# A feed-forward input projection in seven quadrant products in place of eight, on one Trainium2 core

## The reference, cut to what matters

```
def swiglu(h, w13, w2):
    a, g = jnp.split(h @ w13, 2, axis=-1)     # w13: 1024 x 5632
    return (jax.nn.silu(g) * a) @ w2          # w2: 2816 x 1024

def ffn_sublayer(x, mod, j, g_pre, g_post, w13, w2):
    h = modulate_in(x, g_pre, mod, j)
    return gated_residual(x, swiglu(h, w13, w2), g_post, mod, j, 0.5)
```

## Time and profile before

| | |
|---|---|
| median of 3 runs | 2567.58 us (2563.26 to 2568.49) |
| span of the profiled execution | 2563.5 us; its own device time is not listed apart from the three above |
| PE busy | 2506.9 us, 98% of the span |
| DVE, ACT, POOL busy | 57%, 27%, 6% |
| granted TensorE clock, mean | 0.995 |
| last feed-forward block on PE | from 2089.6 us to the last matmul at 2556.3 us |

### The profile page before, as it was taken

The page is one execution under the profiler, slowest core; times in us unless marked ns, Lnnn a source line. Parts: engine busy times, 40 slices in busy tenths (PEclk is TensorE's granted clock), DMA queues, the critical chain, the costliest instruction groups (busy, mean ns, idle before and its releaser), DMA issues. The chain is left out here.

```text
span 2563.5 us, 40540 instructions
## 1 busy us (share of the span) xinstructions
PE 2506.9 (98%) x15408; PEld 2327.2 (91%) x15408; DVE 1454.7 (57%) x2575; ACT 696.8 (27%) x1262; POOL 163.0 (6%) x263
## 2 busy tenths in 40 slices
PE   6999999999998999999999999999999999999998
PEld 5998999799888799989988998999899989989997
DVE  4887688734555688738867884333544453323333
ACT  4111111443445431111124111122421252111122
POOL 0000000201115100000001000000200020000001
PEclk9999999999999999999999999999999999999999
DMA  6553455333223244334442542223122312222232
GB/s 242 156 143 128 132 151 176 92 77 83 51 56 87 79 134 147 122 106 148 147 157 70 151 135 97 79 75 117 55 68 74 116 50 74 65 80 77 74 114 74
DMA packets 383576, 273.14 MB, mean 107 GB/s; under 512 B 39254, under 2 KB 354390, under 8 KB 382454
## 3 DMA queue, kind: packets, MB, share of 16 engines
q1 hardware_dynamic: 383478, 271.82, 35.3%
HBM read 267.42 MB, written 4.32 MB: 106 GB/s over the span
## 5 line engine op out<-in xcount | busy, mean ns | idle before, releaser
L1603 DVE TENSOR_TENSOR w_lo<-w_raw,w_hi 128x1024 fp32r<-128x1024 f32 (+1 forms) x401 | 398.2, 996 | 611.9 <-ACT w_hi L1130 607.4
L809 PE MATMUL psum<-hT_hi,w_hi 128*128 128x320 f32 x3040 | 692.8, 309 | 2.2 <-DVE w_lo L1603 1.4
L809 PE MATMUL psum<-hT_hi,w_lo 128*128 128x320 f32 x3040 | 692.8, 309 | 0.0
L809 PE MATMUL psum<-hT_lo,w_hi 128*128 128x320 f32 x3040 | 692.7, 309 | 0.0
L1130 ACT ACTIVATE w_hi<-w_raw 128x1024 fp32r<-128x1024 f32 (+1 forms) x401 | 349.3, 873 | 957.9 <-PE psum L809 535.8
L809 PEld LDWEIGHTS psum<-hT_hi,w_hi 128*128 128x128 f32 x3040 | 508.4, 188 | 3.7 <-issue 1.5
L809 PEld LDWEIGHTS psum<-hT_hi,w_lo 128*128 128x128 f32 x3040 | 508.4, 188 | 0.0
L809 PEld LDWEIGHTS psum<-hT_lo,w_hi 128*128 128x128 f32 x3040 | 508.0, 188 | 0.0
L1572 DVE SCALAR_TENSOR_TENSOR mod_acc<-ada_raw,cond_silu,mod_acc 128x256 f32<-128x256 f32 x896 | 365.3, 478 | 0.0
L736 PE MATMUL psum<-w_hi,act_hi 128*128 128x512 f32 x800 | 317.8, 397 | 2.8 <-DVE w_lo L1603 2.2
L737 PE MATMUL psum<-w_lo,act_hi 128*128 128x512 f32 x800 | 316.2, 395 | 0.0
(11 more groups left out here) (212 smaller groups left out, 2351.7 us busy)
## 6 DMA issues: line engine op xcount, KB each, us to landing
w_raw<-in_ffn_w_dram SPq DMA_DIRECT2D x176, 512.0 KB, 4.1
ada_raw<-in_ada_w_dram SPq DMA_DIRECT2D x128, 512.0 KB, 3.6
w_raw<-in_ffn_w_dram SPq DMA_DIRECT2D x148, 256.0 KB, 2.8
w_raw<-in_ab_w_in_dram SPq DMA_DIRECT2D x28, 512.0 KB, 4.0
w_raw<-in_sc_w_in_dram SPq DMA_DIRECT2D x24, 512.0 KB, 4.0
ada_first<-in_ada_w_dram SPq DMA_DIRECT2D x4, 2048.0 KB, 18.8
held_raw<-in_ffn_w_dram SPq DMA_DIRECT2D x28, 256.0 KB, 3.7
gate<-modulation SPq DMA_DIRECT2D x6, 1024.0 KB, 6.3
```

Of the source, the lines that this page charges most:

```text
L809: last = mm(IN[p][0:width, h, 0:HT], a, b[:, k, h * HT:(h + 1) * HT], start=(k == 0 and a is hi and b is hT_hi), stop=(k == KD - 1 and a i ...
L1603: V.tensor_tensor(d_, a, b.bitcast(F32), ALU.subtract).then_inc(w_lo_ok, 1)
```

## The change

In the last feed-forward block 3 of the 22 pairs stay as they were (the first three of the first half) and 19 are done in another form, called groups here, 8 in the first half and 11 in the second. The two units of a pair are taken as a 2x2 block matrix (unit by half of the 1024 inputs, each quadrant 4 slices of 128x128), the activations as another (half of the inputs by half of the tokens). Winograd's form of Strassen's product needs 7 products of quadrants, each 4 x 3 = 12 matmuls of 320 columns, and sums before and after.

- **Sums of the weights**: 4 a group, 128x512 on DVE (`weight_sums`). The split becomes 7 copies of 128x512 on ACT (`prod_split`) and 7 subtractions of 128x512 on DVE (`prod_rest`).
- **Sums of the activations**: once, beside the 3 plain pairs: 2 additions of 128x1280 on POOL, 6 sums and 4 subtractions on DVE, 4 copies on ACT.
- **Sums of the results**: of the 7 products, 3 go on top of a bank that holds an earlier one. ACT copies product 0 out (`keep_one`), DVE adds product 1 (`add_two`), product 2 (`add_five`) and product 3 (`add_seven`), then adds into the two crossing quarters (`cross`). Silu is two ACT instructions of 320; then one product, one copy and one subtraction of 640.
- **Waits on PE**: product 4 waits for `add_two` of its own group, product 5 for `add_five`, product 6 for `add_seven`.
- **Memory**: the activation sums take the place of `X`. x is written to device memory (5 transfers of 512 KB) beside the second plain pair and read back in the last output projection. The gate tile's place holds the first three products' weights, so the gate rows are loaded only after the last product.

Of the two loops over `g` in the diff the first is ACT's, the second DVE's.

```diff
+            def pair_products(s, ph, g):
+                b = banks(ph, g)
+                new = g - ph["g0"]
+                for q in range(SEVEN):
+                    pe.wait_ge(prod_lo_ok, SEVEN * g + q + 1)
...
+                    elif q == 4:
+                        pe.wait_ge(q_summed, U_TWO(g))
+                    elif q == 5:
+                        pe.wait_ge(q_summed, U_FIVE(g))
+                    else:
+                        pe.wait_ge(q_summed, U_SEVEN(g))
+                    out = PS[:, b[ACCUM[q]], 0:HT]
...
+                    for k in range(KH):
+                        on = dict(skip_group_check=q >= 4)
+                        mm(out, hi[:, k, :], o_hi[:, k, :], start=(k == 0 and q < 4), stop=False, **on)
+                        mm(out, hi[:, k, :], o_lo[:, k, :], start=False, stop=False, **on)
+                        last = mm(out, lo[:, k, :], o_hi[:, k, :], start=False, stop=(k == KH - 1), **on)
+                    last.then_inc(pe_prod, 1)
...
+            def prod_split(ph, g, q):
+                act.wait_ge(pair_loaded[g % 2][0 if q in (0, 4) else 1], 16 * (g // 2 + 1))
+                if SUMS[q]:
+                    act.wait_ge(ws_ok, 4 * g + SUMS[q])
+                need(act, pe_prod, SEVEN * (g - 1) + q + 1 if g else 0)
...
+                A(prod_hi(q), FACTOR[q](g), ACT.Copy).then_inc(prod_hi_ok, 1)
...
+                for g in range(g0, g1):
+                    more = g + 1 < g1
+                    if more:
+                        prod_split(ph, g + 1, 0)
+                    if g > g0:
+                        keep_hi(ph, g - 1)
+                        keep_one(ph, g)
+                    if more:
+                        for q in (1, 2, 3):
+                            prod_split(ph, g + 1, q)
+                    silu_one(ph, g)
+                    if more:
+                        for q in (4, 5, 6):
+                            prod_split(ph, g + 1, q)
+                    else:
+                        split(ph["nout"], shape="out", prod=slot_done(ph, 0))
+                    silu_two(g)
+                keep_hi(ph, g1 - 1)
...
+            def weight_sums(g, q):
+                if q == 1:
...
+                    V.tensor_tensor(S1[:], A21(g), A22(g), ALU.add).then_inc(ws_ok, 1)
+                    dve.wait_ge(ws_ok, 4 * g + 1)
+                    V.tensor_tensor(S2[:], S1[:], A11(g), ALU.subtract).then_inc(ws_ok, 1)
+                elif q == 3:
+                    V.tensor_tensor(A21(g), A11(g), A21(g), ALU.subtract).then_inc(ws_ok, 1)
+                elif q == 5:
+                    V.tensor_tensor(S2[:], A12(g), S2[:], ALU.subtract).then_inc(ws_ok, 1)
...
+                for g in range(g0, g1):
+                    more = g + 1 < g1
+                    if more:
+                        prod_rest(g + 1, 0)
+                        weight_sums(g + 1, 1)
+                    if g > g0:
+                        product(g - 1)
+                    if more:
+                        prod_rest(g + 1, 1)
+                    if g > g0:
+                        keep_lo(ph, g - 1)
+                        add_two(ph, g)
+                    if more:
+                        prod_rest(g + 1, 2)
+                    if g > g0:
+                        add_five(ph, g)
+                    if more:
+                        weight_sums(g + 1, 3)
+                        prod_rest(g + 1, 3)
+                    add_seven(ph, g)
+                    if more:
+                        prod_rest(g + 1, 4)
+                        weight_sums(g + 1, 5)
+                        prod_rest(g + 1, 5)
+                    else:
+                        split(ph["nout"], shape="out")
+                    cross(ph, g)
+                    if more:
+                        prod_rest(g + 1, 6)
+                product(g1 - 1)
+                keep_lo(ph, g1 - 1)
```

More of the change, by code:

```diff
@@ L80 @@
 LATE = (3, 0)
-UB = [sum(COUNT[k] for k in SUBS[:s]) for s in range(len(SUBS) + 1)]
+units_of = lambda s: COUNT[SUBS[s]] - (2 * (2 * HF - sum(PLAIN[s])) if s in PLAIN else 0)
+UB = [sum(units_of(q) for q in range(s)) for s in range(len(SUBS) + 1)]
 class Steps:
@@ L1093, in _ @@
                 for z, ph in enumerate(plan[s]):
-                    if kind == "ffn":
+                    if s in PLAIN:
+                        for i in range(1, ph["plain"]):
+                            in_unit(ph, 0, i, 2)
+                            in_unit(ph, 1, i, 2)
+                        for g in range(ph["g0"], ph["g1"]):
+                            pair_products(s, ph, g)
+                        out_phase(s, ph, ACT_HI, ACT_LO)
+                    elif kind == "ffn":
                         if z:
@@ L1233, in out_splits @@
                 for u in range(AB_SPLIT if ph.get("ab") else 1, len(units)):
-                    split(ph["nout"] + u, shape="out", u=u)
+                    split(ph["nout"] + u, shape="out", u=u, prod=slot_done(ph, u) if seven(ph) and u < 4 else 0)
                     for i in range(ph["held"]):
@@ L1240, in out_splits @@
                         square_out(s, 0, t)
-                if not final:
+                elif s in PLAIN:
+                    for q in range(3):
+                        prod_split(plan[s][1], plan[s][1]["g0"], q)
+                else:
                     split(ph["nout"] + len(units))
+            def prod_split(ph, g, q):
[3 more added lines that the diff above has]
+                need(act, pe_prod, SEVEN * (g - 1) + q + 1 if g else 0)
+                if g == ph["g0"] and q >= 3:
+                    act.wait_ge(pe_unit, slot_unit(ph, q))
+                A(prod_hi(q), FACTOR[q](g), ACT.Copy).then_inc(prod_hi_ok, 1)
@@ new lines, in t_split, with keep_one @@
+            def t_split(s, ph, i):
+                act.wait_ge(t_sum, 6 * FI[s] + (2, 3, 4, 6)[i])
+                if i in (1, 2):
+                    act.wait_ge(y_stored, 16 * NT * (FI[s] + 1))
+                if i == 3:
+                    act.wait_ge(pe_unit, ph["nout"])
+                A(T_HI[i], tsum[i][:], ACT.Copy).then_inc(t_hi, 1)
+            def keep_one(ph, g):
+                act.wait_ge(pe_prod, SEVEN * g + 1)
+                if g:
+                    act.wait_ge(q_summed, U_CROSS(g - 1))
+                A(U2[:], PS[:, banks(ph, g)[0], 0:HT], ACT.Copy).then_inc(q_gated, 1)
@@ new lines, in silu_one, with silu_two, keep_hi @@
+            def silu_one(ph, g):
+                act.wait_ge(pe_prod, SEVEN * g + 5)
+                if g > 0:
+                    act.wait_ge(q_summed, U_PRODUCT(g - 1))
+                A(Z[:, 0, :], PS[:, banks(ph, g)[0], 0:HT], ACT.Silu).then_inc(q_gated, 1)
+            def silu_two(g):
+                act.wait_ge(q_summed, U_CROSS(g))
+                A(Z[:, 1, :], Z[:, 1, :], ACT.Silu).then_inc(q_gated, 1)
+            def keep_hi(ph, g):
+                act.wait_ge(q_summed, U_PRODUCT(g))
+                j = HF - ph["g1"] + g
+                A(halves(act_hi[:, j, :]), Z[:, 2:4, :], ACT.Copy).then_inc(q_gated, 1)
@@ new lines, in mixed_in @@
+            def mixed_in(s, ph):
+                nb, g0, g1 = ph["nin"], ph["g0"], ph["g1"]
+                for i in range(ph["plain"]):
+                    if i:
+                        split(nb + 1 + 2 * i)
+                    if i == ph["plain"] - 1:
+                        for q in range(3):
+                            prod_split(ph, g0, q)
+                    act.wait_ge(pe_unit, nb + 1 + 2 * i)
+                    need(act, in_evac[(nb + 1) % 2], inv(ph, nb + 1) - 1 + i)
+                    A(halves(sg[:]), IN_V[nb % 2], ACT.Silu).then_inc(in_evac[nb % 2], 1)
+                    if i + 1 < ph["plain"]:
+                        split(nb + 2 + 2 * i)
+                    for z in {0: (1, 0), 1: (2,)}.get(i, ()):
+                        t_split(s, ph, z)
+                for q in range(3, SEVEN):
+                    prod_split(ph, g0, q)
+                    if q == 4:
+                        keep_one(ph, g0)
+                if ph["plain"]:
+                    t_split(s, ph, 3)
+                for g in range(g0, g1):
[16 more added lines that the diff above has]
+                keep_hi(ph, g1 - 1)
```

253 lines of the change are left out of this document (244 added, 9 removed).

## The result

The changed kernel takes **2590.31 us** (median of 4 runs, 2588.36 to 2592.17), the kernel before 2566.24 us beside it (4 runs, 2563.26 to 2568.49): ratio 1.0092, interval 1.0078 to 1.0106, or 24.1 us slower. The profiled execution took 2588.83 us, its span is 2587.0 us.

The account below looks back on a forecast made before the run. The prediction took PE's matmuls to bound the last block. Terms -33.4 + 32.3 + 3.3 + 8.0 + 4.5 + 4.5 = +19.2 us put the median at 2586.8, stated as 2586; range 2563 to 2608.

Parts of the forecast that it names:

- fewer matmuls: PE in 19 groups: 84 matmuls for 96 at 0.1467 us each, 19 x 1.76 = 33.4 us less.
- steady stall: Product 4 waits 2.15 us for add_two in all groups but each half's first and last: 15 times, 32.3 us.
- plain pairs: Second plain pair's value unit: weights late behind the activation sums, a stall of 3.3 us, bounds 0 and 5.
- first groups: First group of each half: product 6 late behind add_seven, 4.8 us in the first half, 3.2 in the second.
- output projections: Output unit 1's weights late, 1.3 us twice, and unit 2's in the last half, 1.9: 4.5 us, bounds 1 and 10.
- clock: Clock at 0.50 after the 3.2, 3.3 and 4.8 us stalls: three spells of some 1.5 us, 4.5; bounds 0 and 27.
- the formula of the Trainium skill: Price of a matmul of 320 columns: columns over 2.4 GHz plus 2.5 ns, 136 ns, making the gain 31.0 us.
- The listing of engine steps: Steady group step by step on PE, DVE and ACT: product 4 at 9.19 us for 7.04, group lasting 14.47 us.
- The 1.9 at unit 2: Last output projection: unit 2's weights, behind gate rows taking up to 7.6 us, ready at 10.3 for 8.4 wanted.
- The rival of a clock that falls at nearly every stall: Clock spells at nearly every stall of the last block add 27 us: +42 in all, 2609 us; chance 12%.
- The rival of a hidden chain: In steady groups add_two is ready at 7.04, the 15 stalls go, 17.6 us are won: 2550 us; chance 13%.

Follow-up runs that it names:

- experiment 6: Kernel before, with the last 2 of 8 value-unit slices left out in 19 pairs (84 matmuls for 96): 2530.76 us, ratio 0.9863.
- experiment 1: Changed kernel, with add_two moved on DVE ahead of the weight rest and the 640 subtraction: 2573.44 us, ratio 1.0037 to the kernel before.
- experiment 2: As experiment 1, and ACT copies product 0 out ahead of the 640 copy: 2569.05 us, ratio 1.0018 to the kernel before.
- experiment 3: Changed kernel, with all of a group's ACT and DVE instructions reordered, none removed: 2539.23 us, ratio 0.9902 to the kernel before.
- experiment 4: experiment 3, plus output unit 1's split earlier, POOL's two additions on DVE, activation sums behind the second pair's weights: 2532.78 us, ratio 0.9874.
- experiment 7: Changed kernel, with POOL's two 128x1280 additions made by DVE ahead of its own sums: 2594.46 us, ratio 1.0105 to the kernel before.
- experiment 8: Changed kernel, with each of POOL's two 128x1280 additions cut into four of 128x320: 2591.74 us, ratio 1.0096 to the kernel before.
- experiment 10: Changed kernel, with output unit 1's split made ahead of the last pair's results in each half: 2589.72 us, ratio 1.0098 to the kernel before.
- experiment 5: experiment 4's kernel, with output unit 2's weights issued ahead of the gate rows in the last output projection: 2533.09 us, ratio 0.9867.

## Why the prediction was right, and where it was not

The sign, the mechanism and the place were right; the forecast of 2586 is 4 us short, 4.9 by the sums. In the sum one term is 9.4 short and three others are 4.5 too large together, so that part of the nearness is luck.

| term of the sum | forecast | measured |
|---|---|---|
| fewer matmuls | -33.4 | -33.4 (experiment 6) |
| steady stall | 15 x 2.15 = 32.3 | 15 x 2.08 = 31.2 |
| plain pairs | 3.3 | 2.2 |
| first groups | 4.8 + 3.2 | 4.6 + 3.1, with restart 8.0 |
| output projections | 4.5 | 2.2 |
| clock | 4.5 | 13.9 |
| sum | 19.2 | 24.1 (stage: 24.9) |

- **PE's work.** As the row of the trace said, and not as the formula of the Trainium skill.
- **The steady stall.** The listing of engine steps named the right place (product 4), the right releaser (`add_two`) and the right size: the group lasts 14.40 us, forecast 14.47 (where no spell falls in it). That it is the order and not DVE's load is shown by experiments 1 to 3: the same instructions in another order leave no wait. DVE's share of the two input projections, 69 and 68% of the windows, would not have told.
- **Plain pairs.** The stall came from two causes and I had one. I forecast the weights late behind the chain of sums (experiment 4, which moves the sums, removes that stall; experiment 7, which leaves them, does not). I did not forecast the first stall: a DVE instruction held up by POOL's additions. POOL's second addition ended at 2100.57 + 5.84 = 2106.41, and DVE's at 2107.50, 1.09 later, about its own duration alone. That is what "SBUF — State Buffer" of the Trainium skill, section "SBUF: two separate sides", describes: DVE with two inputs in the on-chip memory and GpSimd reading there exclude each other for a whole instruction. Experiment 7 agrees (no addition on POOL, 1.23 us), and the transfers that I had as a rival cause are out, as none was under way; by this rule experiment 8 should have cost up to a piece, 0.97 us, and it cost nothing. I had weighed no such rule. That POOL's additions of 128x1280 cause the delay is shown; that a lock held for a whole instruction is how, is not.
- **First groups.** Right, and removed by experiment 3.
- **Output projections.** Unit 1 was 1.08 for 1.3. The 1.9 at unit 2 did not show: the gate rows took 5.7 us to land for the 7.6 of the earlier trace rows, and the late unit 1 covered the rest. Experiment 10 takes that cover away and finds 1.34.
- **The clock, the mis-sized term.** The step that failed: "After 2.30 us of idle PE the granted clock stood at 0.50 (1.2 GHz); after 2.03 us it stayed at 1.00. My steady stalls of 2.15 lie between", from which I took three spells, 4.5 us. Nine units came, 13.9 us. Of the three places where I had put one, two had it: the plain pairs (behind the stall that I had not forecast) and the first half's first group, there twice as long. The stalls were also set on the wrong scale: 2.15 is what a stall adds to the period, and 2.30 and 2.03 are idle times as the profile gives them. Where the period grew by 2.08 the profile has 1.87 idle, so 2.15 answers to about 1.94 (an estimate, 2.15 - 0.21), under both rows, and by them no steady stall should have had a spell. Six of the fifteen, of 1.87 us, were followed by one. Nor is the length of the stall what decides: at the very stall of 2.03 us in the earlier trace rows that left the clock at 1.00, experiment 7's kernel, which has the same code there, shows

```profile
827.72 0.46 PE L1217 MATMUL psum<-vm_tok,scoresT 128*128 128x129 f32 x2 [2.03 <-DVE h_sum L2422]
```

```profile
829.00:833.00 4.00, 2.08 (x10) 1.82 (x10) 2.17 (x8) 3.17 (x17) 3.78 (x5) 0.50 0.01 2
```

and in experiment 8's kernel the stall of 3.09 us in the second half's first group was followed by none, as in the changed kernel:

```profile
2355.65 0.39 PE L963 MATMUL psum<-hT_hi,w_hi 128*128 128x320 f32 x1 [3.09 <-DVE z_quarters L2109]
```

```profile
2357.00:2360.00 3.00, 3.00 (x23) 3.00 (x22) 2.02 (x3) 2.02 (x4) 0.00 (x0) 1.00 0.00 0
```

A stall's length gives odds only. Which stall gets a spell stays open; the runs show that with two waits of 0.4 a group none followed them (experiment 1), and that with none of the large stalls the input projections had none (experiment 4) or one, at the block's first matmuls (experiment 5). The rival of a clock that falls at nearly every stall, 2609, had the right cause and too large a count.
- **The rival of a hidden chain** (2550) was wrong for the order as written, and right of the form: given another order, the seven products win their 33 us.

## What to carry to other kernels

When matmuls are traded for work on DVE and ACT, don't add up shares; list one period instruction by instruction, with the handovers, as each engine's order has it, and look for a result that PE awaits behind an instruction that waits for another engine. Then try the order before giving up the trade: here it was worth 51 us with nothing removed, twice what the change had lost. Count each recurring stall of PE at its length and a share of a clock spell on top, here 13.9 us for 21 stalls, and compare stalls on one scale, either as idle time or as what they add to the period.

## What the runs showed of the hardware

- The granted clock fell to 0.50 (1.2 GHz) for 3.4 us behind idle stretches of PE of 1.87 us, at 6 of 15 that were alike; each spell cost 1.55 us, and it hid as much of a stall close behind it (the second plain pair: 0.28 us with a spell before it, 1.82 in experiment 10 without).
- A DVE subtraction of 128x1024 took 3.66 us for 1.23 beside POOL's 128x1280 addition, and 1.23 beside POOL's 128x320 pieces. Why the pieces did not hold it at all stays open; POOL's records are rough.
- 5 MB more of transfers beside the last output projection cost nothing that could be measured (ratio 1.0004, 0.9994 to 1.0013).
